# Attention heads in pairs: one fused instruction for mask, scale and maximum

## The reference, cut to what matters

```python
def swa_sink_attention(h, w_q, q_norm, sinks, w_o, k_win, v_win, mask, cos, sin):
    ...
    scale = HEAD_DIM ** -0.5
    def block_attn(args):
        qi, ki, vi, mi = args
        s = jnp.einsum('bqkgd,bskd->bkgqs', qi, ki).astype(F32) * scale
        s = jnp.where(mi[None, None, None], s, -jnp.inf)
        sink_col = jnp.broadcast_to(sink[None, :, :, None, None], s.shape[:-1] + (1,))
        p = jax.nn.softmax(jnp.concatenate([s, sink_col], axis=-1), axis=-1)[..., :-1]
        return jnp.einsum('bkgqs,bskd->bqkgd', p.astype(vi.dtype), vi)
    ...
    return o @ w_o
```

## Time and profile before

| what | value |
|---|---|
| median of 3 runs | 1569.38 us (1566.95 to 1570.19) |
| the profiled execution's own time | 1568.28 us |
| its span, first to last instruction | 1566.5 us |
| mean granted TensorE clock | 0.959 of full speed |
| busy shares of the span | PE 94%, DVE 83%, ACT 63%, POOL 4% |
| HBM traffic | 309 GB/s over the span |
| the heads: first L1136 to end of the last L759 | 480.8 to 530.1 us |

### The profile page before, as it was taken

One profiled execution on the slowest core, in us unless ns is written; L12 is line 12 of the kernel. 1 busy time (PEld: TensorE's weight loads), 2 busy tenths in 40 slices (PEclk: granted clock), 3 DMA queues, 4 the chain that ended last, 5 costly groups with the idle time before them and its releaser, 6 DMA issues.

```text
span 1566.5 us, 18974 instructions
## 1 busy us (share of the span) xinstructions
PE 1479.6 (94%) x7463; PEld 1236.6 (79%) x7464; DVE 1293.1 (83%) x1547; ACT 989.4 (63%) x1184; POOL 66.3 (4%) x57
## 2 busy tenths in 40 slices
PE   6897699999898979999999999999999999999996
PEld 6675599999644777888888888888888888888885
DVE  6729788888657738879999999999999999999995
ACT  1251244344325328868888888888888888888884
POOL 0000000000000003001001001000000000100100
PEclk7997799999997979999999999999999999999998
DMA  9954759989841247989999999999999999999980
GB/s 340 324 211 145 273 178 318 326 308 327 318 161 54 75 167 265 380 309 370 385 389 365 384 392 366 378 393 363 384 393 374 375 394 356 383 394 366 382 314 15
DMA packets 222158, 485.44 MB, mean 310 GB/s; under 512 B 6160, under 2 KB 33008, under 8 KB 222064
## 3 DMA queue, kind: packets, MB, share of 16 engines
q1 hardware_dynamic: 217296, 474.04, 82.3%
q0 software_dynamic: 2160, 7.87, 2.0%
q10 hardware_dynamic: 2608, 2.27, 0.4%
HBM read 477.86 MB, written 6.29 MB: 309 GB/s over the span
## 4 chain that ended last, share of the span: by engine, by line
issue 51%; PE 35%; DVE 8%; POOL 3%; ACT 2%; DMA 1%; SPq 0%; ACTq 0%; DVEq 0%; POOLq 0%
PE bank L1373 5%; PE bank L1406 5%; PE bank L1407 4%; PE bank L1408 4%; PE bank L1607 3%; PE bank L1609 3%; PE bank L1608 3%; PE bank L1466 2%; DMA ring<-in_ada_w 1%; PE bank L1357 1%; POOL y L579 1%; POOL out L583 1%; DVE sqb L920 1%; PE bank L1446 1%; PE bank L1340 1%
## 5 line engine op out<-in xcount | busy, mean ns | idle before, releaser
L1245 DVE TENSOR_TENSOR wlo<-ring,whi 128x1024 fp32r<-128x1024 f32 x672 | 814.4, 1235 | 76.6 <-ACT whi L835 55.2
L835 ACT ACTIVATE whi<-ring 128x1024 fp32r<-128x1024 f32 x672 | 711.8, 1062 | 176.9 <-PE bank L1609 176.7
L1607 PE MATMUL bank<-whi,xh 128*128 128x512 f32 x904 | 359.4, 398 | 4.0 <-DVE wlo L1245 3.8
L1609 PE MATMUL bank<-wlo,xh 128*128 128x512 f32 x904 | 353.7, 391 | 0.0
L1608 PE MATMUL bank<-whi,xl 128*128 128x512 f32 x904 | 353.1, 391 | 0.0
L1607 PEld LDWEIGHTS bank<-whi,xh 128*128 128x128 f32 x904 | 170.4, 188 | 41.0 <-issue 7.6
L1609 PEld LDWEIGHTS bank<-wlo,xh 128*128 128x128 f32 x904 | 170.2, 188 | 36.5
L1608 PEld LDWEIGHTS bank<-whi,xl 128*128 128x128 f32 x904 | 170.6, 189 | 33.6
L1607 PE MATMUL bank<-whi,hh 128*128 128x512 f32 x440 | 172.2, 391 | 0.0
L1609 PE MATMUL bank<-wlo,hh 128*128 128x512 f32 x440 | 171.3, 389 | 0.0
L1608 PE MATMUL bank<-whi,hl 128*128 128x512 f32 x440 | 171.2, 389 | 0.0
(11 more groups left out here) (252 smaller groups left out, 1647.1 us busy)
## 6 DMA issues: line engine op xcount, KB each, us to landing
ring<-in_m_w_gu SPq DMA_DIRECT2D x112, 2048.0 KB, 11.8
ring<-in_m_w_down SPq DMA_DIRECT2D x56, 2048.0 KB, 10.9
ring<-in_ada_w SPq DMA_DIRECT2D x24, 2048.0 KB, 14.7
ring<-in_f_w_gu SPq DMA_DIRECT2D x24, 1024.0 KB, 13.4
ring<-in_f_w_down SPq DMA_DIRECT2D x6, 2048.0 KB, 14.5
ring<-in_a_w_in SPq DMA_DIRECT2D x4, 2048.0 KB, 21.0
ring<-in_kv_ada_w SPq DMA_DIRECT2D x4, 2048.0 KB, 12.2
ring<-in_a_w_out SPq DMA_DIRECT2D x2, 2048.0 KB, 12.0
```

The source lines that it names most:

```text
L835: nc.scalar.activation(whi[:, n % WB, :], moe_raw(n), ACT.Copy).then_inc(hi_ready, 1)
L1245: v_.tensor_tensor(wlo[:, n % WB, :], moe_raw(n), whi[:, n % WB, :].bitcast(F32), ALU.subtract).then_inc(lo_ready, 1)
L1607: mm(o, hi, whi[:, b, c0:c0 + 512], start=start, stop=False)
L1609: return mm(o, hi, wlo[:, b, c0:c0 + 512], start=False, stop=stop)
```

## The change

The heads are worked on as 8 pairs `p`, heads `2p` and `2p + 1`.

- DVE: scale, mask and maximum become one instruction, `tensor_tensor_reduce`, which writes the masked scores and the row maximum and starts the maximum from the sink. There are four for a pair (two heads, 128 and 256 columns), with no wait between them. Negation is one instruction for the pair; a new one adds the sinks to it (`es_set`).
- DVE: sum, inverse and scaling are done for a pair at once. The scaling is a `tensor_tensor` against a broadcast inverse, where it was a `tensor_scalar`.
- ACT: a pair's four exponentials follow each other without waits, one instruction serves the sinks of the pair, one copies both heads' transposes (768 columns).
- The copy of a finished pair moves from ACT to DVE.
- PE: `scores(p)` holds three fillers and then the four products, ordered so that the even head's and the odd head's stand next to each other, in different banks. For a pair there are three fillers where there were four.
- PSUM is one tensor of 8 banks; score tiles use 4 banks, transposes 2 banks for one pair at a time, outputs 2 banks. The masked scores have three places of a pair each, where there were four of a head.
- DVE does `scores(p + 2)`, `probs(p)`, `copy_o(p - 1)`. PE does `scores(p + 2)`, `probs_T(p)`, `values(p - 1)`.

```diff
-            for h in range(NH):
-                if h + 2 < NH:
-                    exps(h + 2)
-                copy_p(h)
-                if h >= 2 and h % 2 == 0:
-                    copy_o(h // 2 - 1)
+            for p in range(NH // 2):
+                if p + 1 < NH // 2:
+                    exps(p + 1)
+                copy_p(p)
...
+            def scores(p):
+                dve.wait_ge(sc_mm, p + 1)
+                if p >= 3:
+                    dve.wait_ge(pT_mm, p - 2)
+                pair = slice(2 * p, 2 * p + 2)
+                for j in range(2):
+                    h = 2 * p + j
+                    for c0, c1, i in ((0, P, 0), (P, 3 * P, 1)):
+                        ins = v_.tensor_tensor_reduce(out=Pb[p % 3][:, j, c0:c1], in0=score_bank(p, j)[:, c0:c1],
+                                                      in1=mask[:, c0:c1], scale=HD ** -0.5, scalar=sinks[:, h:h + 1],
+                                                      op0=ALU.add, op1=ALU.max, accum_out=mx[:, h, i:i + 1])
+                then(ins, sce)
+                then(v_.tensor_scalar(nm[:, pair, :], mx[:, pair, :], -1.0, None, ALU.mult), nms)
+                then(v_.tensor_tensor(es[:, pair, :], nm[:, pair, :], sinks[:, pair][:, :, None].to_broadcast([P, 2, 2]),
+                                      ALU.add), ess)
...
+            def probs(p):
+                pair = slice(2 * p, 2 * p + 2)
+                dve.wait_ge(exp_done, p + 1)
+                then(v_.tensor_tensor(sm[:, pair, :], sm[:, pair, :], es[:, pair, :], ALU.add))
+                then(v_.reciprocal(sm[:, pair, :], sm[:, pair, :]))
+                for c0, c1, i in ((0, P, 0), (P, 3 * P, 1)):
+                    ins = v_.tensor_tensor(Pb[p % 3][:, :, c0:c1], Pb[p % 3][:, :, c0:c1],
+                                           sm[:, pair, i:i + 1].to_broadcast([P, 2, c1 - c0]), ALU.mult)
+                then(ins, pns)
+
+            def copy_o(p):
+                dve.wait_ge(pv_mm, p + 1)
+                then(v_.tensor_copy(A[:, p, :], bank[6 + p % 2][:, 0:SEQ]), oe)
+
+            for p in range(2):
+                scores(p)
+            for p in range(NH // 2):
+                if p + 2 < NH // 2:
+                    scores(p + 2)
+                probs(p)
+                if p:
+                    copy_o(p - 1)
+            copy_o(NH // 2 - 1)
...
-            for h in range(3):
-                scores(h)
-                keep_clock()
-            for h in range(NH):
-                if h + 3 < NH:
-                    scores(h + 3)
-                for _ in range(2):
-                    keep_clock()
-                probs_T(h)
-                if h:
-                    values(h - 1)
-            values(NH - 1)
+            for p in range(2):
+                scores(p)
+            for p in range(NH // 2):
+                if p + 2 < NH // 2:
+                    scores(p + 2)
+                probs_T(p)
+                if p:
+                    values(p - 1)
+            values(NH // 2 - 1)
```

More of the change, by code:

```diff
@@ L739, in _ @@
             copy_T(5)
[L741 to L749, removed]
@@ L1127, in _ @@
                     ada(25)
[L1129 to L1140, removed]
@@ L1151, in _ @@
-            for h in range(NH):
-                if h + 2 < NH:
-                    scores(h + 2)
-                probs(h)
+            sce, nms, ess, pns, oe = (Signal(sc_evac), Signal(nm_done), Signal(es_set), Signal(pn_done),
+                                      Signal(o_evac))
+            def scores(p):
[3 more added lines that the diff above has]
+                pair = slice(2 * p, 2 * p + 2)
+                for j in range(2):
+                    h = 2 * p + j
+                    for c0, c1, i in ((0, P, 0), (P, 3 * P, 1)):
[6 more added lines that the diff above has]
+                                      ALU.add), ess)
@@ L1470, in _, with scores @@
             to_T(5)
[L1472 to L1475, removed]
+            def scores(p):
+                if p >= 2:
+                    pe.wait_ge(sc_evac, p - 1)
                 else:
                     pe.wait_ge(qkT_done, 6)
[L1478 to L1481, removed]
@@ L1521, in _ @@
-            values(NH - 1)
+                g = 2 * p // (NH // NKV)
+                half = ones[:, :].bitcast(BF16)
+                for _ in range(3):
+                    mm(score_bank(p, 0)[:, :], ident[:, :].bitcast(BF16)[:, 0:P],
+                       half[:, None, :].to_broadcast([P, 2, 2 * P]), start=True, stop=True)
+                for j in range(2):
+                    lo = HD * j
+                    mm(score_bank(p, j)[:, 0:P], B[lo:lo + HD, p, 0:P], kT[lo:lo + HD, g, 0:P], start=True, stop=True)
@@ new lines, in scores, with probs_T @@
+                for j in range(2):
+                    lo = HD * j
+                    last = mm(score_bank(p, j)[:, P:3 * P], B[lo:lo + HD, p, P:2 * P], kT[lo:lo + HD, g, :], start=True,
+                              stop=True)
+                last.then_inc(sc_mm, 1)
+            def probs_T(p):
+                pe.wait_ge(pn_done, p + 1)
+                if p:
+                    pe.wait_ge(pT_evac, p)
+                for j in range(2):
+                    for i in range(3):
+                        last = transposed(bank[4 + j][:, i * P:(i + 1) * P], Pb[p % 3][:, j, i * P:(i + 1) * P],
+                                          ident[:, :])
+                last.then_inc(pT_mm, 1)
@@ new lines, in values @@
+            def values(p):
+                pe.wait_ge(pT_evac, p + 1)
+                if p >= 2:
+                    pe.wait_ge(o_evac, p - 1)
+                g = 2 * p // (NH // NKV)
+                v0, v1 = vt[:, 0, g * HD:(g + 1) * HD], vt[:, 1, g * HD:(g + 1) * HD]
+                for j in range(2):
+                    o = bank[6 + p % 2][HD * j:HD * j + HD, :]
+                    p_ = PT[:, 2 * (p % 2) + j, :]
+                    mm(o[:, 0:P], v0, p_[:, 0:P], start=True, stop=True)
+                    mm(o[:, P:2 * P], v0, p_[:, P:2 * P], start=True, stop=False)
+                    last = mm(o[:, P:2 * P], v1, p_[:, 2 * P:3 * P], start=False, stop=True)
+                last.then_inc(pv_mm, 1)
```

67 lines of the change are left out of this document (24 added, 43 removed).

## The result

The changed kernel takes 1584.82 us (median of 4 runs, 1583.75 to 1585.78) against 1568.78 us before, 16.0 us more; the ratio is 1.0104, with a 95% interval from 1.0091 to 1.0116. Its profiled execution spans 1583.2 us against 1566.5.

The account below looks back on a forecast made before the run. DVE was taken to set the heads' pace, 5.48 us for two heads. Start to 493.0, turns of 7.95 and 40.2, tail 16.3 end the heads at 557.5 against 530.09: 27.4 us more, 1596 us, range 1577 to 1611.

Parts of the forecast that it names:

- The ring: In the heads, DVE and PE wait for each other and work in turn: 8.3 us a turn against 5.48.
- The clock: PE's clock falls in most pauses of the heads and returns during PE's work: a turn of 10.05 us.
- PE's part: PE's transposes, values, fillers and score products in one turn of the heads: 4.27 us at full clock.
- half of the half-clock cost: Clock allowance in a turn: halfway between 8.3 us at full clock and 11.8 at half, so 10.05.
- Rival 1: Heads' turns at full clock throughout, DVE and PE alternating: 14.7 us more, 1583 us; chance 0.25.
- Rival 2: Heads' turns at half clock throughout, DVE and PE alternating: 1608 us; chance 0.20.
- Rival 3: In the heads, DVE stays the bound and its shorter work sets the pace: 8 us less, 1560 us; chance 0.05.
- The start: Heads up to the first scaling: DVE's first score instruction at 482.8 us, three pairs' scores and first probs done at 493.0.
- The turns: Five turns of pairs 3 to 7: 7.95 us for the first, without values, and 40.2 for four more.
- The tail: End of the heads, after the last scores: 13.0 us at full clock, 16.3 with the clock allowance.
- the fused instructions' price: DVE's four fused score instructions for a pair: 2.1 us, with 0.11 us added for each accumulator write.
- Counting the heads in full: What the heads lose or win reaches the kernel's end in full; later stages change by at most 3 us.

Follow-up runs that it names:

- e1: The changed kernel with PE's look-ahead alone put back: three pairs' scores first, then scores(p+3) ahead of pair p's transposes; 1576.03 us, ratio 1.0047.
- e3: The changed kernel with PE looking ahead three pairs, the output copy on ACT and four places for masked scores instead of three; 1554.03 us, ratio 0.9902.
- e5: The kernel before, single heads, with PE issuing two heads' scores first instead of three, then scores(h+2) instead of scores(h+3); 1619.52 us, ratio 1.0326.
- e4: The changed kernel with 12 more useless fillers for each pair, in PE's pause before the wait for the scaled probabilities; 1574.66 us, ratio 1.0041.
- e8: The changed kernel with PE looking ahead three pairs and the output copy on ACT, still three places for masked scores; 1561.32 us, ratio 0.9956.
- e9: e4 with both heads' score products taken from the even head's half of the rows, odd heads' own scores left out; 1584.68 us, ratio 1.0112.
- e10: The changed kernel without the three fillers in each pair's scores; 1580.93 us, ratio 1.0086.
- e11: e3 without the three fillers in each pair's scores; 1553.47 us, ratio 0.9911.
- e2: The changed kernel with only the copy of a pair's output put back on ACT; 1581.70 us, ratio 1.0079.
- e6: e4 with the score products in the order even 128, even 256, odd 128, odd 256; 1574.84 us, ratio 1.0043.

## Why the prediction was right, and where its numbers were off

Predicted were 1596 us (1577 to 1611), and slower by over 0.2% at 0.92. It came out at 1584.8, inside the range and 11 us below the forecast: 16 us more than before where 27 were forecast.

**The ring** was right and is shown from both sides: the change without it (e1) wins back 9 of the 16 us, and with all three waits gone (e3) it is 31 us faster; the kernel before with it (e5) is 51 us slower. The waits in the trace are the ones named.

**The clock** fell once in every turn, as forecast, though not early in the pauses: it fell near their end, or twice just behind the transposes, and it came back late in PE's part or in the next pause. Its price was right: half of the half-clock cost was 1.75 us a turn, and measured are 8.87 us, the mean of four turns, less e4's 7.07, so 1.8. In all e4 puts it at 10 us. Rival 1's number, 1583, lies nearer to the result than the forecast's, but that is luck: with the clock full in the turns it is 1574.7 (e4), so its ring was 8 us too slow, and the falls that it left out cost 10. Rival 2's clock, at half throughout, came up only in e5.

**Rival 3**, that DVE's shorter work sets the pace, needed PE's longer look-ahead and the copy on ACT. With both the kernel is 7 us faster than before (e8), and with the fourth place too 14 (e3), where I had priced 8.

What the sum had wrong is the size of its terms. Its three parts erred all one way, by 12.8 us in the heads:
- *The start* (to the end of the first scaling, 493.0 predicted, 488.2 measured): 4.8 us. DVE's first fused instruction came at 481.09 instead of 482.8; 1.2 us of that is only that PE's part began earlier in this profile (477.87 against 479.08 before). Then it took 7.1 us instead of 10.2: 1.9 of the difference is the price of three pairs' fused instructions, and 1.2 the half clock that I had assumed until then. The clock rose at about 481.4.
- *The turns*: 7.5 us for the first and 35.5 for four more, against 7.95 and 40.2: 5.1 us. DVE's part is 3.37 instead of 4.03 (the fused four 1.47 instead of 2.1). PE's part at full clock is 3.70 instead of 4.27 (e4): two heads' values take 1.08 us from first load to filler (501.41 to 502.49), not 1.50, and from the first product to DVE's start it is 1.08 us instead of 1.32, so the second head's products are nearly free. Only the fillers were priced too low, 0.75 us measured (502.49 to 503.24) against 0.66.
- *The tail*: 13.5 instead of 16.3 us. At full clock it is 12.4 in e4, where I had 13.0, and the clock cost 1.1 us instead of 3.3.

The largest single error is the fused instructions' price, 0.63 us for each pair. I had added 0.11 us for each accumulator write; the write lies wholly under its neighbours, and the fused instructions themselves overlap, with starts 0.27 us behind a narrow one and 0.40 behind a wide one. The 0.059 us that I called the price of a per-partition scalar came from two rows that differ in more: the dearer one also reads from PSUM, so what costs it isn't shown, though the instructions' own durations came out as priced. Behind the values' price was a row of two heads with a wait between them. Without it, in e4, their loads interleave: the second head's first (501.69) comes before the last product's of the first head (L1534, from 501.80). Counting the heads in full at the end was right within 2 us.

What stays open: what brings the clock back, and so why it rose early in the change's heads and why e9 lost 12 us of full clock there. It isn't the fillers alone: without any it rose at about 480 us in e10 and only at about 493 in e11. Nor is it enough that PE is busy, since its record shows it busy without a gap over 481 to 493 us in e9, at 0.50. No run separated that.

## What to carry to other kernels

When two in-order engines feed each other, compare how far each looks ahead at the point where one waits: if the producer's next work stands behind the wait for the consumer's last, both engines take turns, and a turn costs the sum of their work. Here 3.37 us of DVE and 3.70 of PE made 7.07 even at full clock, where the old order took 5.48 us with more work on DVE. Merging small steps makes this easier to do by accident, since a look-ahead of three heads became one of two pairs on the producer while the consumer's stayed "two". Look at all waits of the loop at once: taking away the first showed the second (the copy behind the transposes) and then the third (the places for scores). The three steps brought 9, 15 and 7 us (e1, e8, e3), and the second alone only 3 (e2), so a wait that costs nothing in one order can be the bound in the next.

## What the runs showed of the hardware

Two heads' score products on opposite halves of the array's rows cost the time of one head's: 0.64 us less a turn than on the same half (e9 against e4), in either order of the four that was tried (e4, e6). The Trainium skill, "TensorE: Matmul & The Clock Gate", Part 3 (Packing small matmuls), says that products on distinct row groups run concurrently and that column groups behave alike; the first agrees with e9. The values' products, which write opposite halves of the output partitions, took 1.08 us for two heads in e4 against 0.80 for one before, which fits the second, though no run isolated it.

DVE's accumulator write took 0.083 us and was hidden, where ACT's is 0.186. And work without use in a pause of TensorE can pay: twelve fillers in the pause of each turn made e4 10 us faster, while the same kind of fillers inside the ring brought no gain that can be seen (e10, without them, is 3 us faster by the ratios, with overlapping intervals).
